# A hybrid diffusion layer: the last twelve gate tiles as seven half-block products a pair, the modulation rows turned later, the first output product waiting per feature tile

## The reference, cut to what matters

```python
h = _rmsnorm(x, norm_mix) * (1 + sc1) + sh1
p = h @ w_in
ya, yb, yc, yd = pool(p), hyena(p), shortconv(p), attention(p)   # widths 256, 256, 256, 512
gates = sigmoid(h @ w_gate + b_gate)                              # width 4 * 1024
merged = ga * (ya @ w_br_a) + gb * (yb @ w_br_b) + gc * (yc @ w_br_c) + gd * (yd @ w_br_d)
x = x + g1 * (merged @ w_out)
h2 = _rmsnorm(x, norm_ffn) * (1 + sc2) + sh2
x = x + g2 * moe(h2)          # 4 groups x 8 experts, top-1 group, top-2 experts
```

## Time and profile before

| | us |
|---|---|
| median of 3 runs (lowest, highest) | 1153.44 (1152.76, 1154.8) |
| the profiled execution | 1152.68 |
| its span, first to last instruction | 1151.0 |
| TensorE busy (matmuls) | 1045.0 |
| VectorE, ScalarE, GpSimd busy | 492.0, 214.0, 207.4 |
| mean granted TensorE clock | 0.955 of full |

### The profile page before, as it was taken

One profiled execution on the slowest core, in us unless ns is written; L12 is line 12 of the kernel. 1 busy time (PEld: TensorE's weight loads), 2 busy tenths in 40 slices (PEclk: granted clock), 3 DMA queues, 4 the chain that ended last, 5 costly groups with the idle time before them and its releaser, 6 DMA issues.

```text
span 1151.0 us, 13981 instructions
## 1 busy us (share of the span) xinstructions
PE 1045.0 (91%) x5263; PEld 629.9 (55%) x5263; DVE 492.0 (43%) x1208; ACT 214.0 (19%) x403; POOL 207.4 (18%) x271
## 2 busy tenths in 40 slices
PE   4999999999999999999999999999967999969670
PEld 2466766876566665666665555445544555535330
DVE  4655676043745645546544111035543322212126
ACT  4110001000243343333400000012200111101002
POOL 3140000010590001111111411112221333222110
PEclk9999999999999999999999999999958999989895
DMA  9921220242342332242232930101399999999956
GB/s 313 371 84 54 73 73 1 101 119 71 96 128 73 110 110 74 74 147 73 74 110 73 366 98 37 37 37 73 114 400 382 398 406 407 407 406 408 406 232 274
DMA packets 100867, 209.84 MB, mean 182 GB/s; under 512 B 8680, under 2 KB 64310, under 8 KB 100672
## 3 DMA queue, kind: packets, MB, share of 16 engines
q1 hardware_dynamic: 87984, 179.19, 42.8%
q0 software_dynamic: 12784, 29.75, 7.2%
q10 hardware_dynamic: 32, 0.01, 0.0%
HBM read 197.86 MB, written 18.79 MB: 188 GB/s over the span
## 4 chain that ended last, share of the span: by engine, by line
PE 82%; DMA 9%; SPq 4%; DVE 3%; issue 1%; ACT 0%; POOLq 0%; DVEq 0%
PE pair L1790 24%; PE pair L1797 13%; PE pair L1789 7%; PE pair L1824 6%; PE pair L2120 6%; PE pair L1793 4%; PE pair L2137 3%; DMA ring_region<-in_w_e_down 3%; PE pair L1946 3%; PE pair L2010 2%; SPq L679 2%; PE pair L1923 2%; DMA hyena_region<-in_w_e_up 2%; DMA hT_region<-in_w_e_up 2%; PE pair L1886 1%
## 5 line engine op out<-in xcount | busy, mean ns | idle before, releaser
L1790 PE MATMUL pair<-hT_region,ring_region 128*128 128x512 f32 x544 | 280.8, 598 | 0.0
L1789 PEld LDWEIGHTS pair<-hT_region,ring_region 128*128 128x128 f32 x544 | 102.3, 192 | 122.3 <-issue 120.6
L1789 PE MATMUL pair<-hT_region,ring_region 128*128 128x128 f32 x544 | 107.2, 279 | 1.8 <-DVE hT_region L1501 1.5
L857 POOL TENSOR_TENSOR dft_region<-dft_region,padded_region 128x640 f32<-128x640 f32 x24 | 37.1, 1544 | 345.1 <-DVE padded_region L1428 345.0
L1790 PEld LDWEIGHTS pair<-hT_region,ring_region 128*128 128x128 f32 x544 | 83.6, 194 | 0.0
L1428 DVE TENSOR_TENSOR padded_region<-pair,padded_region 128x640 f32<-128x640 f32 x24 | 19.8, 825 | 138.5 <-PE pair L2010 95.4
L1824 PE MATMUL pair<-ring_region,dft_region 128*128 128x512 f32 x160 | 73.1, 608 | 3.1 <-issue 2.9
L2120 PE MATMUL pair<-ring_region,padded_region 128*64 128x256 f32 x640 | 73.5, 382 | 0.0
L1722 DVE TENSOR_TENSOR mixer_region<-pair,mixer_region 128x128 f32<-128x128 f32 x34 | 9.9, 291 | 143.8 <-ACT mixer_region L1097 143.8
L1060 ACT ACTIVATE padded_region<-pair,colv 128x640 f32<-128x640 f32 x32 | 25.4, 795 | 232.6 <-PE pair L1790 232.6
L880 POOL DMA_INDIRECT moe_pairs<-padded_region,bias_region x34 | 34.5, 1016 | 188.1 <-DVE padded_region L1736 182.5
(11 more groups left out here) (391 smaller groups left out, 1661.6 us busy)
## 6 DMA issues: line engine op xcount, KB each, us to landing
ring_region<-in_w_ada SPq DMA_DIRECT2D x24, 1024.0 KB, 7.3
ring_region<-in_w_gate SPq DMA_DIRECT2D x16, 1024.0 KB, 5.7
ring_region<-in_w_in SPq DMA_DIRECT2D x13, 1024.0 KB, 5.5
ring_region<-in_w_e_gate SPq DMA_DIRECT2D x12, 1024.0 KB, 13.6
ring_region<-in_w_e_up SPq DMA_DIRECT2D x12, 1024.0 KB, 18.5
ring_region<-in_w_e_down SPq DMA_DIRECT2D x24, 512.0 KB, 16.3
hT_region<-in_w_e_gate SPq DMA_DIRECT2D x7, 1024.0 KB, 13.6
hT_region<-in_w_e_up SPq DMA_DIRECT2D x7, 1024.0 KB, 17.6
```

The costliest lines, as they stand in the source:

```text
L857: pool.tensor_tensor(merged[:, dj, :], merged[:, dj, :], gtmp, ALU.add).then_inc(merged_add, 1)
L1789: mm(ps_[0:m, W0:W0 + TC], lhsT, rhs[:, 0:TC], start=start, stop=stop)
L1790: return mm(ps_[0:m, W0 + TC:1024], lhsT, rhs[:, TC:T], start=start, stop=stop)
```

## The change

Gate tiles 20 to 31 are made in pairs (`GPAIRS` = 20, 22, ..., 30). The steps `("gate", ...)` of these tiles are gone; a pair has four steps: gp (products A11·B11 and A12·B21), gm (S1·T1 and S2·T2), gn (S3·T3 and S4·B22) and gq (A22·T4). The two branch products of the pair stand behind them. VectorE makes the four input differences behind the last attention step (O of n = 19), in the region that the reloaded `x1` takes later, and the weight sums of a pair behind gn of the pair before. It mixes the products into the two gate buffers, and ScalarE takes the sigmoid there in place. The halves of modulation weights of n = 21 and 22 are now summed behind the merge of tile 20 and the mixing of gp(22), their parts stand between gm and gn of pair 22 and behind its gq. The step `rows` moves behind gq(24). SP reloads `x1` only behind gq(30) and the output weights, with a semaphore for the context rows and one for the latent rows. The first output product waits for the adds of each feature tile by itself.

```diff
+GPAIRS = list(range(4 * NT, len(BRANCHES) * KD, 2))
...
-            s += [("gate", b, dj)]
-
-            if n - 1 in HALVES:
+            if n in GPAIRS:
+                s += [("gp", n), ("gm", n)]
+                s += [("part",) + HALVES[n - 1]] if n - 1 in HALVES else []
+                s += [("gn", n), ("gq", n)]
+                s += [("part",) + HALVES[n]] if n in HALVES else []
+                s += [("rows",)] if n == 3 * KD else []
+            elif n < GPAIRS[0]:
+                s += [("gate", b, dj)]
+
+            if n - 1 in HALVES and n < GPAIRS[0]:
                 s += [("part",) + HALVES[n - 1]]
...
-        if b == 2:
-            s += [("rows",)]
...
+    if k in ("gp", "gm", "gn", "gq"):
+        n = step[1]
+        early = [("ada",) + HALVES[i] for i in (n, n + 1) if i in HALVES] if k == "gp" else []
+        return early + [("gate", n // KD, n % KD // 2)]
...
-                if name == ("branch", 3, 1):
-
-                    computed(sp, ("O", 4 * NT - 1))
-                    sp.wait_ge(kv_out, 32)
-                    sp.dma_start(x1[:, 0, :], I["x_prompt"][0]).then_inc(x_again, 16)
-                    sp.dma_start(x1[:, 1:NT, :], I["x_sample"][0].rearrange("(t p) d -> p t d", p=P)
-                                 ).then_inc(x_again, 16)
+
+            computed(sp, ("gq", GPAIRS[-1]))
+            sp.dma_start(x1[:, 0, :], I["x_prompt"][0]).then_inc(x_again, 16)
+            sp.dma_start(x1[:, 1:NT, :], I["x_sample"][0].rearrange("(t p) d -> p t d", p=P)).then_inc(x_rest, 16)
...
+                elif k == "gp":
+                    n = st[1]
+                    if n == GPAIRS[0]:
+                        computed(act, ("OT", 4 * NT - 1))
+                    else:
+                        drained(act, ("gq", n - 2))
+                    computed(act, st)
+                    act.activation(kept_g[0], ps(st)[:, 0:HALF], ACT.Copy).then_inc(g_kept, 1)
+                elif k in ("gn", "gq"):
+                    n = st[1] + int(k == "gq")
+                    act.wait_ge(gate_mixed, n - GPAIRS[0] + 1)
...
+                    act.activation(gate[:, n % 2, :], gate[:, n % 2, :], ACT.Sigmoid,
+                                   bias=v_("b_gate")[:, KD * g + dj:KD * g + dj + 1]).then_inc(gate_ready, 1)
...
+            def sum_gate_weights(n):
+                w = loaded(dve, ("gate", n // KD, n % KD // 2)).rearrange("p (k n) -> p k n", k=KD)
+                A11, A12, A21, A22 = quarters(w)
+                S1, S2, S4 = Sg
+                if n > GPAIRS[0]:
+                    computed(dve, ("gn", n - 2))
+                link(tt(S1, A21, A22, ALU.add))
+                put(tt(A21, A11, A21, ALU.subtract))
+                link(tt(S2, S1, A11, ALU.subtract))
+                tt(S4, A12, S2, ALU.subtract).then_inc(g_weight_sums, 1)
+
+            def sum_gate_input():
+                T1, T2, T3, T4 = Tg
+                computed(dve, ("O", 4 * NT - 1))
+                dve.wait_ge(kv_out, 32)
+                link(tt(T1, B12, B11, ALU.subtract))
+                tt(T2, B22, T1, ALU.subtract).then_inc(g_input_sums, 1)
+                sum_gate_weights(GPAIRS[0])
+                tt(T3, B22, B12, ALU.subtract).then_inc(g_input_sums, 1)
+                dve.wait_ge(g_input_sums, 2)
+                tt(T4, B21, T2, ALU.subtract).then_inc(g_input_sums, 1)
+
+            def mix_gates(st):
+
+                k, n = st
+                left, right = ps(st)[:, 0:HALF], ps(st)[:, 512:512 + HALF]
+                s, y = kept_g
+                one, two = (gate[:, i, :] for i in range(2))
+                computed(dve, st)
+                if k == "gp":
+                    dve.wait_ge(g_kept, GPAIRS.index(n) + 1)
+                    frees(tt(one[:, 0:HALF], right, s, ALU.add), st)
+                elif k == "gm":
+                    drained(dve, ("gp", n))
+                    link(tt(s, right, s, ALU.add))
+                    frees(tt(y, left, s, ALU.add), st)
+                elif k == "gn":
+                    drained(dve, ("gm", n))
+                    tt(one[:, HALF:T], right, y, ALU.add).then_inc(gate_mixed, 1)
+                    put(tt(two[:, HALF:T], left, y, ALU.add))
+                    dve.wait_ge(gate_mixed, n - GPAIRS[0] + 1)
+                    own.wait()
+                    frees(tt(s, left, s, ALU.add), st)
+                else:
+                    drained(dve, ("gn", n))
+                    put(tt(two[:, 0:HALF], left, s, ALU.add))
+                    own.wait()
+                    dve.sem_inc(gate_mixed, 1)
+                    dve.sem_inc(psum_free[AT[st] % 4], 1)
+                drained(dve, st)
...
+                    if st[1] == 4 * NT - 1:
+                        sum_gate_input()
+                elif k in ("gp", "gm", "gn", "gq"):
+                    mix_gates(st)
+                    n = st[1]
+                    if k == "gp" and n in HALVES:
+                        sum_half(*HALVES[n])
+                    elif k == "gn" and n < GPAIRS[-1]:
+                        sum_gate_weights(n + 2)
...
+                    n = st[1] * KD + st[2]
+                    if n in GPAIRS and n + 1 in HALVES:
+                        sum_half(*HALVES[n + 1])
...
-                        dve.wait_ge(x_again, 32)
+                        dve.wait_ge(x_again, 16)
                         computed(dve, ("shift",))
+                    if (k, t) == ("oa", 1):
+                        dve.wait_ge(x_rest, 16)
...
+                    if t == 0 and half == 0:
+                        pe.wait_ge(merged_add, 2 * KD + kt + 1)
...
+                    if k == "gp":
+                        product(left, A11, B11)
+                        ins = product(right, A12, B21)
+                    elif k == "gm":
+                        pe.wait_ge(g_weight_sums, GPAIRS.index(n_) + 1)
+                        pe.wait_ge(g_input_sums, 1)
+                        product(left, S1, T1)
+                        ins = product(right, S2, T2)
+                    elif k == "gn":
+                        pe.wait_ge(g_input_sums, 2)
+                        product(left, S3, T3)
+                        ins = product(right, S4, B22)
+                    else:
+                        pe.wait_ge(g_input_sums, 3)
+                        ins = product(left, A22, T4)
...
-                    if t == 0:
-                        pe.wait_ge(merged_add, 3 * KD)
```

More of the change, by code:

```diff
@@ L475, in build @@
         kept = [[x[:, HALF * i:HALF * (i + 1)] for i in range(2)] for x in (RQ[:, 3968:3968 + 640], RP[:, 3840:3840 + 640])]
+        Tg = [x1[:, 0:5, :].rearrange("p t d -> p (t d)")[:, quarter * i:quarter * (i + 1)]
+              .rearrange("p (k t) -> p k t", k=KD // 2) for i in range(4)]
+        Sg = [x.rearrange("p (k m) -> p k m", k=KD // 2) for x in (RD[:, 5120:5632], RD[:, 5632:6144], RP[:, 1760:2272])]
+        kept_g = [RP[:, 4480 + HALF * i:4480 + HALF * (i + 1)] for i in range(2)]
         def late(t):
@@ L608, in build @@
             sem(n) for n in ("input_sums", "weight_sums", "product_kept"))
+        x_rest = sem("x_again_latent")
+        g_input_sums, g_weight_sums, g_kept, gate_mixed, gate_ready = (
+            sem(n) for n in ("gate_input_sums", "gate_weight_sums", "gate_product_kept", "gates_mixed", "gates_ready"))
         flags_counted, further_turned = sem("further_counted"), sem("further_listed")
@@ L1061, in _ @@
                                          bias=v_("b_gate")[:, KD * g + dj:KD * g + dj + 1]), st)
+                elif k == "gp":
[9 more added lines that the diff above has]
+                    act.wait_ge(gate_mixed, n - GPAIRS[0] + 1)
+                    b, dj = n // KD, n % KD
+                    g = BRANCHES[b][1]
+                    act.activation(gate[:, n % 2, :], gate[:, n % 2, :], ACT.Sigmoid,
+                                   bias=v_("b_gate")[:, KD * g + dj:KD * g + dj + 1]).then_inc(gate_ready, 1)
                 elif k == "oa":
@@ L1419, in merge @@
                 computed(dve, st)
-                drained(dve, ("gate", b, dj))
+                if n < GPAIRS[0]:
+                    drained(dve, ("gate", b, dj))
+                else:
+                    dve.wait_ge(gate_ready, n - GPAIRS[0] + 1)
                 if b == 0:
@@ L1982, in _ @@
                     ins = turn(p_[:, 0:P], orow)
+                elif k in ("gp", "gm", "gn", "gq"):
+                    n_ = st[1]
+                    left, right = p_[:, 0:HALF], p_[:, 512:512 + HALF]
+                    w = loaded(pe, ("gate", n_ // KD, n_ % KD // 2)).rearrange("p (k n) -> p k n", k=KD)
+                    A11, A12, S3, A22 = quarters(w)
+                    S1, S2, S4 = Sg
+                    T1, T2, T3, T4 = Tg
+                    if k == "gp":
[10 more added lines that the diff above has]
+                        ins = product(right, S4, B22)
+                    else:
+                        pe.wait_ge(g_input_sums, 3)
+                        ins = product(left, A22, T4)
```

## The result

The changed kernel takes **1140.01 us** (median of 4 runs, 1139.14 to 1140.37); the kernel before took 1153.66 beside it (4 runs, 1152.76 to 1154.8). The ratio is 0.988, 95% interval 0.9863 to 0.9897: 13.7 us faster. The forecast was 1138.3 with a range of 1134.0 to 1143.0.

The account below looks back on a forecast made before the run. TensorE's own work was taken to bound the last gate tiles. Terms -13.4 - 2.57 - 1.7 + 1.3 + 0.6 + 0.7 = -15.1 us took the profiled 1152.68 to 1137.6, as a median 1138.3; range 1134 to 1143.

Parts of the forecast that it names:

- Products: Six gate-tile pairs, seven half-block products each: 15.07 us instead of 17.31, saving 2.24 a pair, 13.4 us in all.
- Place 4: First output product, at the end: the 2.57 us wait goes, and the slow stretch behind it, another 1.7 us.
- Place 1: Pair 20, behind attention: TensorE waits for VectorE's sums before gm, +1.3 us; +1.7 more if the clock falls.
- after the 0.86 us one the pace stayed: Pair 20: the clock held behind TensorE's 0.86 us pause, so a 1.3 us wait was taken to cost no clock.
- Place 2: Pair 22: TensorE waits for VectorE's half of the modulation weights before the second part, +0.6 us (0 to 2).
- the rule: VectorE and GpSimd share an SBUF port pair exclusively; each weight sum meeting a GpSimd add would cost up to 1.3 us.
- Place 3: Modulation rows, moved behind gq(24): TensorE waits 3.75 us instead of 3.0, +0.7 us (-4.7 to +3); clock falls as before.
- rival A: The new waits are longer or cost clock: about +3 us, 1141.5; chance 0.17.
- B: The wait before the modulation rows gets short enough to keep the clock, or vanishes: -4.5 us, 1134; chance 0.08.
- C: The output-product gain is taken back by transfers behind gq(30) or a wait at the eighth feature tile: +4.3, 1142.6; chance 0.07.
- D: Slower: hand-overs between TensorE and VectorE pace every pair, some 8 us each: +33 us, 1186; chance 0.04.
- E: No change: new waits take what the seven-product pairs save, 1153 us; chance 0.02.

Follow-up runs that it names:

- five pairs: The changed kernel with gate tiles 20 and 21 single again and the first weight sums behind merge 21: 1141.36 us, ratio 0.9893.
- the wait put back: The changed kernel with the first output product again waiting for all 24 adds at once: 1143.86 us, ratio 0.9915.
- early gather: The changed kernel with VectorE gathering the six modulation rows right behind the last part (11,1), their turning left behind gq(24): 1133.28 us, repeated at 1133.3.

## Why the prediction was right, term by term

**Products: -13.4, right.** The three groups of the last branch took 15.07 to 15.13 us, and TensorE's busy time fell by 14.4. No run takes the products out and leaves the rest, so this term rests on these rows; five pairs, the nearest run, would give back 2.24 us and showed 1.5, within the noise.

**Place 4: -2.57 and -1.7, right in that trace.** The 2.57 us went and the record is 1.77 us shorter. By the medians the part is worth 3.7 alone and 3.85 on top, not 4.27. The noise is wide enough for 4.27; a slow stretch that is not in every execution would also do it, and the trace of the wait put back has none, but this is not shown.

**Place 1: +1.3, measured +1.77 here and 1.1 to 1.24 elsewhere.** VectorE's walk came out as worked out. VectorE's timeline, first and last sum before gm:

```profile
585.02 1.49 DVE L1480 TENSOR_TENSOR qkv_region<-hT_region 128x1280 f32<-128x1280 f32 x1
...
590.00 0.69 DVE L1474 TENSOR_TENSOR padded_region<-ring_region,dft_region 128x512 f32<-128x512 f32 x1
```

They end at 590.69, 5.4 us after TensorE resumes; I had 5.6. Where the clock holds, gm starts 593.29 - 587.89 = 5.40 us after gp, 1.1 more than the 4.30. Where it falls, gp itself takes 6.07 and hides the wait. I had the fall as an addition to the wait (1.3 + 1.7); it comes instead of it. The step that failed is "after the 0.86 us one the pace stayed": one trace was read as a rule, and the pause that the clock fell behind was that one, not the new wait.

**Place 2: +0.6, measured 1.06.** The two halves took 7.43 us (607.04 to 614.47) and 7.26 (615.97 to 623.23), where I had 7.4 each. Both met an add of GpSimd. The timelines of GpSimd and of VectorE, at the second half:

```profile
615.62 1.53 POOL L874 TENSOR_TENSOR dft_region<-dft_region,padded_region 128x640 f32<-128x640 f32 x1 [6.84 <-DVE padded_region L1463]
```

```profile
615.97 1.33 DVE L1528 TENSOR_SCALAR hyena_region<-ring_region,scT 128x256 f32<-128x256 f32 x1
617.34 0.35 DVE L1528 TENSOR_SCALAR ring_region<-ring_region,scT 128x256 f32<-128x256 f32 x1
```

The same operation takes 1.33 us beside the add and 0.35 behind it. The half that I had read in the kernel before contains such a meeting too, in a line between those shown:

```profile
599.37 1.51 DVE L1442 TENSOR_SCALAR ring_region<-ring_region,scT 128x256 f32<-128x256 f32 x1
```

So the meeting was in my 7.4 us without my having seen it. It explains most of the wait (without the second one, 0.98 us less, some 0.1 would be left), but not what the forecast missed. Missing were the pauses in which VectorE waits for its own last write: 0.24 us between the first half and the merge, 0.21 between the second half and gm's mixing; I had nothing for either. The part started 0.22 us later than in my walk (624.52, I had 624.3), and TensorE was there 0.24 us earlier (623.46, I had 623.7). The Trainium skill (SBUF — State Buffer, "SBUF: two separate sides") has this case too: the lock also holds off a VectorE operation that uses both ports for one source. The traces agree: the instruction ends 0.15 us behind the add. In the changed kernel's two traces the weight sums, for which I had weighed the rule, never met an add; in the kernel with five pairs one did, and paid 1.22 us.

**Place 3: +0.7, measured +1.2; the reason was right.** This is VectorE's part of the chain that ended last, between gq(24)'s products and the rows (start, length, what):

```profile
643.37 0.49 DVE padded_region L1503
...
644.89 0.70 DVE dft_region L1471
645.59 0.02 issue
645.61 0.69 DVE ring_region L1472
646.30 0.61 DVE dft_region L1473
...
647.55 0.50 DVE padded_region L1510
...
648.38 0.17 DVE mod L1665
648.55 0.07 DVE mod L1666
```

The weight sums for pair 26 and gq's mixing stand ahead of the rows, and the walk from 643.37 to 648.05 is 4.68 us where I had 4.65. Two hand-overs were too short in my sum: VectorE starts 0.61 us after gn's pitch ends at 642.76 (I took 0.25; why it is 0.61 in both traces of this kernel, and 0.25 with the early gather, stays open), and 0.33 us pass between 648.05 and 648.38, in which it waits for its own write and signals it (I took nothing). I counted instructions and not what lies between them. The bound of -4.7 (wait and slow stretch gone) was not reached by moving the step. The early gather reached it, and somewhat more since the wait had grown: what had to move was the producing instructions, not the consuming one.

GpSimd's sends began at 650.43, but waited 1.50 us for the first transfer and not 4.95 as in the kernel before, so that its next add started at 662.26 and not 665: more slack than I gave it.

**Sum.** -13.4 - 2.57 - 1.77 + 1.77 + 1.06 + 1.2 = -13.7; the stage shows -13.65, and the medians -13.7. That these agree so closely is luck: in the second trace of this kernel the stage took 160.96 us, -12.4, since the slow stretch at the rows is twice as long (0.9 us) and the gate weights of pair 20 come late (0.35). I had -15.1: the 1.4 us are the three new waits, each 0.5 short. That is rival A's direction (waits longer, clock lost) at about half its size; B, C, D and E did not occur.

**Open:** why the clock falls behind a pause of 0.86 us in some executions and holds in others of the same kernel, why it held once behind 2.62, and why the slow stretch at the rows lasts 3.4 us in one trace and 6.8 in another.

## What to carry to other kernels

On an engine that works in order, a step that another engine waits for is as late as everything queued before it: moving the waiting step later bought 1.5 us at best guess, within the noise; moving the eight small producing instructions earlier bought 6.7. Replacing eight block products by seven gave its whole gain here, and the waits that the additions brought went once these came in the order in which TensorE asks for them. A duration read from a trace can hold a meeting with another engine: look at the lines inside a sum before using it as a price. Where a stage's border is one wait for all parts, a wait for each part takes the wait off the path (3.7 us here) without any other change.

## What the hardware showed that I had not expected

- TensorE's granted clock fell to 1.2 GHz behind a pause of 0.86 us: of two traces of one kernel in the one (a mean of 0.81 over 9 us) and not in the other (1.00). It held behind a pause of 2.62 us, but fell behind one of 2.57 in the kernel before.
- A VectorE operation of one tensor input, 128x256, took 1.33 to 1.51 us beside GpSimd's add, and 0.35 alone; one of two inputs, 128x512, took 1.91 us and 0.69.
- Where VectorE waited for its own last write, 0.21 to 0.42 us passed before its next instruction (four places of the changed kernel's trace).
